# One 128x128 block-diagonal matrix per chunk for both heads in the chain of RWKV states

## What is computed

```python
def step(S, inp):
    r_t, w_t, k_t, v_t, a_t, b_t = inp
    sa = jnp.einsum('nhvk,nhk->nhv', S, a_t)
    S = S * w_t[:, :, None, :] + sa[..., None] * b_t[:, :, None, :] + v_t[..., None] * k_t[:, :, None, :]
    return S, jnp.einsum('nhvk,nhk->nhv', S, r_t)
```

## Time and profile before

| what | value |
|---|---|
| median of three runs | 3053.57 us (3053.49 to 3055.62) |
| the profiled execution's own time | 3049.05 us |
| its span, first to last instruction | 3047.5 us |
| mean granted TensorE clock | 0.986 of 2.4 GHz |
| PE busy | 2939.7 us, 96% |
| VectorE busy | 1718.7 us, 56% |
| ScalarE busy | 1070.4 us, 35% |
| one RWKV turn | about 117 us, 16 of them from 942 us on |

### The profile page before, as it was taken

The page is one execution under the profiler, slowest core; times in us unless marked ns, Lnnn a source line. Parts: engine busy times, 40 slices in busy tenths (PEclk is TensorE's granted clock), DMA queues, the critical chain, the costliest instruction groups (busy, mean ns, idle before and its releaser), DMA issues. The chain is left out here.

```text
span 3047.5 us, 79337 instructions
## 1 busy us (share of the span) xinstructions
PE 2939.7 (96%) x33831; PEld 2739.7 (90%) x33831; DVE 1718.7 (56%) x2530; ACT 1070.4 (35%) x1802; POOL 405.0 (13%) x811
## 2 busy tenths in 40 slices
PE   7999999999997999999999999999999999997997
PEld 6998998988987999999899899899999999996997
DVE  5455545645655566566476476565575665665323
ACT  4332423323323334243243243243243243333332
POOL 5001001001013012012022022021021021120100
PEclk8999999999998999999999999999999999998998
DMA  5224324325232222222122222132132222222522
GB/s 156 78 70 153 93 70 153 106 65 180 70 118 87 61 70 73 59 72 72 52 72 66 58 75 71 44 86 71 45 79 59 65 73 61 70 71 83 169 84 91
DMA packets 368510, 255.32 MB, mean 84 GB/s; under 512 B 19380, under 2 KB 347568, under 8 KB 366256
## 3 DMA queue, kind: packets, MB, share of 16 engines
q1 hardware_dynamic: 342560, 184.18, 22.0%
q0 software_dynamic: 25600, 66.02, 6.8%
HBM read 212.69 MB, written 37.45 MB: 82 GB/s over the span
## 5 line engine op out<-in xcount | busy, mean ns | idle before, releaser
L204 PE MATMUL psum<-act_hi,w_hi 128*128 128x280 f32 (+1 forms) x4672 | 1427.1, 305 | 15.3 <-DVE w_lo L190 8.4
L205 PE MATMUL psum<-act_lo,w_hi 128*128 128x280 f32 (+1 forms) x4672 | 1362.9, 292 | 0.7 <-issue 0.7
L206 PE MATMUL psum<-act_hi,w_lo 128*128 128x280 f32 (+1 forms) x4672 | 1363.5, 292 | 0.0
L204 PEld LDWEIGHTS psum<-act_hi,w_hi 128*128 128x128 f32 (+1 forms) x4672 | 880.4, 188 | 74.9 <-issue 37.1
L205 PEld LDWEIGHTS psum<-act_lo,w_hi 128*128 128x128 f32 (+1 forms) x4672 | 880.0, 188 | 5.1 <-issue 1.6
L206 PEld LDWEIGHTS psum<-act_hi,w_lo 128*128 128x128 f32 (+1 forms) x4672 | 880.0, 188 | 0.4 <-issue 0.4
L190 DVE TENSOR_TENSOR w_lo<-raw,w_hi 128x1024 fp32r<-128x1024 f32 (+1 forms) x324 | 396.1, 1222 | 284.3 <-ACT w_hi L182 274.6
L182 ACT CAST w_hi<-raw 128x1024 fp32r<-128x1024 f32 (+1 forms) x324 | 339.7, 1048 | 36.2 <-DMA raw<-in_w_out_dram 15.3
L1699 POOL DMA_DIRECT2D out_s_rwkv_dram<-arena x128 | 77.5, 614 | 1381.1 <-ACT arena L1848 1215.3
L2163 PE MATMUL psum<-arena 64*64 64x64 f32 x9984 | 208.2, 223 | 14.7 <-issue 14.4
L2163 PEld LDWEIGHTS psum<-arena 64*64 64x64 f32 x9984 | 182.7, 134 | 40.4 <-issue 37.5
(11 more groups left out here) (342 smaller groups left out, 3545.0 us busy)
## 6 DMA issues: line engine op xcount, KB each, us to landing
raw<-in_w_in_dram SPq DMA_DIRECT2D x288, 512.0 KB, 4.4
arena<-in_state_gla_dram POOLq DMA_DIRECT2D x32, 512.0 KB, 5.0
out_s_gla_dram<-arena POOLq DMA_DIRECT2D x32, 512.0 KB, 3.8
raw<-in_w_out_dram SPq DMA_DIRECT2D x32, 512.0 KB, 4.6
ob_dram<-arena POOLq DMA_DIRECT2D x16, 280.0 KB, 3.2
arena<-ob_dram POOLq DMA_DIRECT2D x16, 280.0 KB, 4.9
m_dram<-arena POOLq DMA_DIRECT2D x16, 280.0 KB, 2.6
act_lo<-m_dram SPq DMA_DIRECT2D x1, 4200.0 KB, 17.4
```

Source lines behind the costliest of these rows:

```text
L204: pe.matmul(out, hi, act_hi[:, k, cols], start=(k == 0), stop=False)
L205: pe.matmul(out, hi, act_lo[:, k, cols], start=False, stop=False)
L206: mm = pe.matmul(out, lo, act_hi[:, k, cols], start=False, stop=(k == KT - 1))
```

## The change

It does five things. `m_t` becomes eight matrices of 128x128 with head 0's matrix in the upper left and head 1's in the lower right quarter, in a region of its own that nothing else writes. POOL clears this region once before turn 0. VectorE writes the two quarters in two instructions of 64 partitions in place of one of 128, for chunks 1 to 8 only. A step of the chain is one product with the 128x128 matrix, which gives both heads' states at once. The two products of line 2296 move from the head of the chain to behind line 2311.

```diff
-DV, DS, DG = 55, 10, 5
+DV, DS, DG = 56, 10, 5
...
-        m_t, n_t = ar(NC, C), ar(NC, C)
+        n_t = ar(NC, C)
...
         state_out = ar(NC, P)
+        m_t = ar(NF, P)
...
-                for tile in (a_r[:, NF, :], b_k[:, NF, :], v_pad, a8):
+                for tile in (a_r[:, NF, :], b_k[:, NF, :], v_pad, a8, m_t):
                     pool.memset(tile, 0.0).then_inc(mine.sem, 1)
...
-                    tt(m_t, maps[:, :, 0:C], bc(eye2, NC), ADD).then_inc(map_ready.sem, 1)
-                    dve.wait_ge(map_ready.sem, map_ready.next(i))
+                    for h in range(2):
+                        rows, signal = slice(64 * h, 64 * h + 64), map_ready if h else mine
+                        tt(m_t[rows, :, 64 * h:64 * h + 64], maps[rows, 1:NC, 0:C], bc(eye2[rows], NF), ADD).then_inc(signal.sem, 1)
+                        dve.wait_ge(signal.sem, signal.next(i))
...
-                            for h in range(2):
-                                mm(bank[6][head[h], C:C + LAST], uv[:, NF, 64 * h:64 * h + 64], gram[:, NF, h, C:C + LAST], start=True, stop=False,
-                                   skip_group_check=True)
                             pe.wait_ge(r_ready.sem, r_ready.at(i, 1))
                             pe.sem_inc(waited.sem, 1)
...
-                        for h in range(2):
-                            before = n_t[head[h], 0, :] if c == 1 else states[head[h], c - 1, :]
-                            m = mm(bank[2][head[h], 0:C], m_t[head[h], c, :], before, start=True, stop=True)
-                        m.then_inc(s_done.sem, 1)
+                        before = n_t[:, 0, :] if c == 1 else states[:, c - 1, :]
+                        mm(bank[2][:, 0:C], m_t[:, c - 1, :], before, start=True, stop=True).then_inc(s_done.sem, 1)
                         run(2)
...
+                    for h in range(2):
+                        mm(bank[6][head[h], C:C + LAST], uv[:, NF, 64 * h:64 * h + 64], gram[:, NF, h, C:C + LAST], start=True, stop=False,
+                           skip_group_check=True)
```

## The result

The changed kernel took 3021.25 us (median of four runs, 3019.21 to 3023.00), the kernel before 3053.53 us beside it: a ratio of 0.9894 with a 95% interval of 0.9877 to 0.9911, or 32 us less. The profiled execution took 3021.32 us, 27.7 us less than the one of before (3049.05). Two later comparisons, on two chips, gave 0.9903 (0.9889 to 0.9917) and 0.9909 (0.9894 to 0.9924), or 29.6 and 29.0 us. The forecast was 3028.7 us in a range of 3023 to 3041: the sign and the mechanism came as forecast, the size fell just past the range's fast end.

What follows compares the result with a forecast made beforehand. PE's instruction stream was taken as the bound. Fifteen turns at 1.88 less 0.14 us gave 26.1, less 1.0 for the clear and 0.2 for the last turn: 24.9 us gained, 3028.7 us, range 3023 to 3041 (own case 3023 to 3035).

Steps and rivals of the forecast that it cites:

- The bound: Whole turns: a turn lasts as long as PE's instructions take, PE being busy for 464.17 of 468 us in four turns.
- The step: Chain of states: one fused step with its six fill products takes 0.998 us, 0.235 less than now.
- rival 3: Chain step: the 0.335 us gap stays and packing is lost, 15.3 us slower, 3068.9 us; chance 0.07.
- VectorE's loop: Chain step, product to VectorE's line 2038 to next product: some 0.97 us, just under the 0.998 us step.
- Rival 1: Chain step: VectorE's loop becomes the bound; at 1.10 us a step 12.9 us gained, 3040.7 us; chance 0.14.
- The split on VectorE: Line 2020 in two halves: 0.76 us more, 0.44 hidden, r_ready 0.3 us later, covered by fill; costed at nothing.
- The moved product: Line 2296, from the chain's head to behind line 2311: 0.39 us there, net +0.14 us a turn.
- The clear: POOL's clearing of m_t before turn 0, ahead of the third shift buffer's seeding: 1.0 us, paid in full once.
- The last turn: Final turn's chain: two steps gain 0.235 us each, five bare ones lose about 0.10 each; together a 0.2 us loss.
- all of it on the path: Whole kernel: the full 24.9 us shortens the time, since fill's operands come after the chain's end or long before.
- Rival 2: After the chain: PE meets a wait the chain covered and the gain is given back, about 3053.6 us; chance 0.09.
- I take the same gain there: Whole kernel: the profiled execution's 24.9 us gain, from 3049.05 us, is applied unchanged to the median of 3053.57 us.

Runs made afterwards that it cites:

- 128x64 experiment: Changed kernel with each chain product split into two of 128 rows by 64 columns, one per head: 3049.89 us, ratio 1.0009 to the kernel before.
- last experiment: Changed kernel with POOL's clear late and line 2296's, then line 2325's products directly behind the samples' products: 3007.45 us, ratio 0.9870 to the kernel before.

## Why the prediction was right on the mechanism and wrong on the sum

**The bound** was read rightly: PE's stream, not VectorE. PE is busy for 114.44 of 115 us in the mean of four turns after the change (stretches of one turn from 1060 us):

```profile
sum 460.00, PE 457.77 PEld 433.18 DVE 292.96 ACT 166.96 POOL 69.35; mean PE 114.44 PEld 108.29 DVE 73.24 ACT 41.74 POOL 17.34
```

No new wait stands before fill inside the turns 1 to 14 that VectorE or ScalarE ended.

**The step** was sized rightly: 0.998 us forecast, 0.996 measured, 0.235 and 0.237 us gained. That the gap goes with the tile shape was argued from three rows, and the 128x64 experiment shows it: rival 3 fell.

**VectorE's loop** just fits, as argued. In the last turn, where fill has run out, the bare step is 0.94 us, against 0.97 estimated and 0.87 before:

```profile
2759.88 0.41 PE L2304 MATMUL psum<-arena 128*128 128x64 f32 x2 [0.54 <-DVE arena L2041]
2760.82 0.41 PE L2304 MATMUL psum<-arena 128*128 128x64 f32 x2 [0.54 <-DVE arena L2041]
```

Rival 1 fell by a margin of 0.05 us a step. In the late step of turn 9 that margin was not enough, and the chain lost 0.3 us. A late start of this kind, by 0.35 us, stands once in each of the twelve traces: in turn 9 wherever VectorE has the changed program, also in the run with PE's code shifted, and in turn 13 of the kernel before, where steps of 1.23 us hid it. It goes with VectorE's program, then; why it comes is open.

**The split on VectorE** cost nothing. The two halves take 1.41 us, line 2026 (2023 of before) follows at once, where it had waited 0.44 us for PE, and the update that signals r_ready ends at 1027.20, ahead of the chain's weight load at 1027.68:

```profile
1024.21 1.41 DVE L2023 TENSOR_TENSOR arena<-psum,arena 64x512 f32<-64x512 f32 x2 [2.52 <-PE psum L2277]
1025.66 0.76 DVE L2026 TENSOR_TENSOR arena<-psum,arena 128x576 f32<-128x576 f32 x1
1026.45 0.75 DVE L2029 TENSOR_TENSOR arena<-arena,psum 128x576 f32<-128x576 f32 x1
```

**The moved product** costs net 0.40 - 0.25 = +0.15 us a turn, forecast +0.14. This holds beside a chain that gains 0.235 us in all eight steps; the experiment that put it back shows that in front of the fused chain it would cost 0.07 us a turn more than behind line 2311. **The clear** made ScalarE wait 0.86 us longer and the first stretch of turn 0 last 0.4 to 0.6 us longer, forecast 1.0: not all of it was on the path. **The last turn** lost 0.9, 0.5 and 0.1 us in the three pairs of traces, forecast 0.2: five bare steps at 0.07 each, and the moved products, which stretch that turn's tail by 0.6 us. These terms add up to 15 x 1.76 - 0.5 - 0.5 = 25.4 us, where the forecast had 24.9; the misses of the clear and the last turn partly cancel, which is luck.

**What failed is the sum**, in two places. The first is "all of it on the path". The three pairs of profiled executions differ by 27.7, 27.4 and 27.0 us (3049.05 to 3021.32, 3046.88 to 3019.52, 3044.78 to 3017.80), not by 24.9. The reason given beside it speaks of fill's operands alone; PE's pauses by "issue" in the dense 64x64 stretch were put at nothing without a reason. They lay in the trace of before (line 2163, 14.4 us), and the change moves them because a turn has 32 fewer PE instructions in the trace. Their sum fell by 3.1, 3.8 and 2.1 us in the three pairs, 3.0 in the mean; that the places moved is shown, while the size rests on three traces of each kernel, of which single ones overlap (17.4 before, 19.7 after). A loss of 0.6 to 0.8 us in the tail of turn 2 went as well, and turn 9 gave 0.3 back. Rival 2, a wait that takes the gain back, did not come: PE lost less for other reasons than before. Where the change touches nothing, the part ahead of the turns took 1.9 to 4.4 us longer and the part behind them 1.1 to 2.5 us less, in sum 1.4 us longer; why is open. With this the means add up: 25.4 + 3.0 + 0.4 - 1.4 = 27.4 us.

The other place is "I take the same gain there", from a profiled execution 4.5 us under the median of its kernel. The changed kernel's median was no higher than its profiled execution, so these 4.5 us came on top of the 27.7 in the first comparison. In the two later comparisons the kernel before had medians of 3048.7 and 3046.4, its unchanged copies 3048.2 and 3042.4, and the gain was 25.0 to 29.6 us. So the first comparison's last 3 us or more belong to how the kernel before ran there. Why it ran longer there is not settled: its medians lie between 3042.4 and 3053.5, those of the changed kernel between 3017.4 and 3021.3. Either miss alone would have left the time inside the range (3053.6 - 27.7 = 3025.9, and 3053.6 - 24.9 - 4.5 = 3024.2); a low end of 3023 had no room for both.

## What to carry to other kernels

Before pricing a small product by its shape, look at the distance from its neighbours on PE: a group in another tile shape between full-size products cost 0.33 us here beyond its own work, more than four packed pieces (0.12 us) took. Where small products alternate with full-size ones, padding them to the full shape can win although half the array multiplies zeros; where they stand in a row, the rows price packing lower (0.12 us for four pieces, 0.22 us for the fused product; not run here). Products of one shape are best put side by side, as the last experiment shows. A chain of dependent steps can then be shortened only until the loop through the other engine takes over, here at 0.94 us. And a gain that was worked out within one profiled execution carries the spread of its kernel: here the median lay 4.5 us above the execution that was read.

## What was not expected of the hardware

PE's instruction stream itself has pauses, and the code's place decides where they can stand. In the dense stretch of 64x64 products they come at multiples of 256 PE instructions, about 5 us apart there, at 19 and 13 places in the first traces of the kernel before and the changed one, and last up to 1.2 us each. Over the 16 turns they cost 15 to 23 us in the six traces of the two kernels. The instruction queue brought 275 packets of 16.4 KB for the kernel before and 273 after, and in the trace of before a packet landed 1.2 to 1.6 us ahead of the end of each of these pauses. That they follow from late instruction packets is the reading that fits, not shown: PE's loads, products and semaphore instructions are some 270 times 256 before (69,165) and 268 times after (68,653), two fewer, as the packets are. Shown is that they go with the code's place (the count of 256, the shift by 100 instructions, and equal places at equal counts). An edit of a few instructions in an unrolled loop can so move the time at places that it does not touch, here by some 3 us in the mean.
